# Four tiles of u move from the choice to the stretch behind the gates; scores of two groups stay in SBUF; ScalarE forms the factors of fetched slots

## The reference, cut to what matters

```python
def _peer(h, w_q, sub_keys, u_tab, v_tab):
    t = h.reshape(-1, d)                                  # 512 tokens x 1024
    qry = (t @ w_q).reshape(n_tok, 8, 2, 128)
    scores = jnp.einsum("thpd,hpkd->thpk", qry, sub_keys) # 128 keys per half
    s_top, i_top = lax.top_k(scores, 16)
    cand = s_top[:, :, 0, :, None] + s_top[:, :, 1, None, :]
    best, pos = lax.top_k(cand, 16)                       # 16 experts of 16384 per head
    gate = jax.nn.softmax(best, axis=-1)
    u = u_tab[ib]
    act = jax.nn.gelu(jnp.einsum("td,thkd->thk", tb, u))
    vv = v_tab[ib]
    return jnp.einsum("thk,thkd->td", gb * act, vv)
```

## Time and profile before

| What | us |
|---|---|
| Median of three runs (3891.67 to 3894.0) | 3893.79 |
| The profiled execution's own time | 3893.74 |
| Its span, first to last instruction | 3891.9 |
| PE busy in the span | 3771.2 (97%) |
| DVE busy | 2111.6 (54%) |
| POOL busy | 1978.0 (51%) |
| ACT busy | 1399.0 (36%) |

### The profile page before, as it was taken

One profiled execution on the slowest core, in us unless ns is written; L12 is line 12 of the kernel. 1 busy time (PEld: TensorE's weight loads), 2 busy tenths in 40 slices (PEclk: granted clock), 3 DMA queues, 4 the chain that ended last, 5 costly groups with the idle time before them and its releaser, 6 DMA issues.

```text
span 3891.9 us, 57381 instructions
## 1 busy us (share of the span) xinstructions
PE 3771.2 (97%) x21920; PEld 3290.5 (85%) x21920; DVE 2111.6 (54%) x3552; ACT 1399.0 (36%) x2131; POOL 1978.0 (51%) x1520
## 2 busy tenths in 40 slices
PE   8999999999999999999999978999999987999998
PEld 7888778888888887788877767889999987999998
DVE  3212555220322056432124855439899968999997
ACT  4222253222322133432232433334477722333332
POOL 4444424444444442444443322546644465888885
PEclk9999999999999999999999988999999998999999
DMA  3222212222222221222223210234456699888885
GB/s 140 97 97 100 77 64 98 97 97 97 95 94 94 104 88 58 92 92 97 98 103 76 44 36 24 99 108 157 154 206 209 226 381 357 326 319 324 323 319 189
DMA packets 160292, 570.02 MB, mean 146 GB/s; under 512 B 19456, under 2 KB 85248, under 8 KB 105344
## 3 DMA queue, kind: packets, MB, share of 16 engines
q1 hardware_dynamic: 49392, 351.29, 25.7%
q10 hardware_dynamic: 96912, 115.76, 8.7%
q0 software_dynamic: 13824, 100.67, 6.3%
HBM read 510.93 MB, written 56.66 MB: 146 GB/s over the span
## 4 chain that ended last, share of the span: by engine, by line
issue 34%; POOL 26%; PE 24%; DVE 13%; ACT 1%; ACTq 1%; DMA 0%; POOLq 0%; DVEq 0%
POOL w_lo L563 25%; PE bank L1362 7%; PE bank L1364 7%; PE bank L1363 7%; DVE g_buf L3043 3%; DVE hot_parts L3025 2%; DVE hot_first L3026 1%; DVE hot_parts L3031 1%; DVE bank L3126 1%; DVE late_factor L3122 1%; DVE fetched L3116 1%; POOL fetched L657 1%; ACT w_hi L730 1%; DVE gk L2601 0%; PE bank L1904 0%
## 5 line engine op out<-in xcount | busy, mean ns | idle before, releaser
L563 POOL TENSOR_TENSOR w_lo<-raw,w_hi 128x512 fp32r<-128x512 f32 x1324 | 1807.6, 1396 | 1722.4 <-ACT w_hi L730 1695.0
L1362 PE MATMUL bank<-h_hi,w_hi 128*128 128x512 f32 (+1 forms) x3232 | 1235.9, 382 | 35.8 <-POOL w_lo L563 22.9
L1363 PE MATMUL bank<-h_lo,w_hi 128*128 128x512 f32 (+1 forms) x3232 | 1222.1, 378 | 0.0
L1364 PE MATMUL bank<-h_hi,w_lo 128*128 128x512 f32 (+1 forms) x3232 | 1222.1, 378 | 0.0
L730 ACT ACTIVATE w_hi<-raw 128x2048 fp32r<-128x2048 f32 x331 | 632.7, 1911 | 832.0 <-PE bank L1364 765.4
L1362 PEld LDWEIGHTS bank<-h_hi,w_hi 128*128 128x128 f32 x3232 | 609.9, 189 | 132.5 <-POOL w_lo L563 34.1
L1363 PEld LDWEIGHTS bank<-h_lo,w_hi 128*128 128x128 f32 x3232 | 610.1, 189 | 89.7 <-issue 3.4
L1364 PEld LDWEIGHTS bank<-h_hi,w_lo 128*128 128x128 f32 x3232 | 609.4, 189 | 88.8
L1362 PE MATMUL bank<-w_mix_hi,w_hi 128*128 128x416 f32 x1024 | 363.3, 355 | 16.0 <-DVE w_mix_lo L3071 15.0
L1364 PE MATMUL bank<-w_mix_hi,w_lo 128*128 128x416 f32 x1024 | 361.8, 353 | 0.0
L1363 PE MATMUL bank<-w_mix_lo,w_hi 128*128 128x416 f32 x1024 | 358.9, 350 | 0.0
(11 more groups left out here) (430 smaller groups left out, 4416.4 us busy)
## 6 DMA issues: line engine op xcount, KB each, us to landing
raw<-weights SPq DMA_DIRECT2D x331, 1024.0 KB, 4.8
s_store<-stage ACTq DMA_DIRECT2D x64, 416.0 KB, 4.7
g_store<-g_buf ACTq DMA_DIRECT2D x8, 3328.0 KB, 15.4
g_in<-g_store ACTq DMA_DIRECT2D x32, 832.0 KB, 6.7
s_in<-s_store ACTq DMA_DIRECT2D x32, 832.0 KB, 8.2
x<-x_in SPq DMA_DIRECT2D x4, 512.0 KB, 8.5
out<-x SPq DMA_DIRECT2D x8, 256.0 KB, 2.2
q_mask<-rows ACTq DMA_DIRECT2D x6, 256.0 KB, 4.3
```

The source lines that it names most:

```text
L563: pool.tensor_tensor(w_lo[:, slot, cols], raw[:, slot, cols], w_hi[:, slot, cols].bitcast(F32), ALU.subtract).then_inc(lo_written, 1)
L1362: pe.matmul(out_ap, w_hi[:, slot, cols], m_hi, start=start, stop=False)
L1363: pe.matmul(out_ap, w_hi[:, slot, cols], m_lo, start=False, stop=False)
L1364: return pe.matmul(out_ap, w_lo[:, slot, cols], m_hi, start=False, stop=stop)
```

## The change

Three things change, all in the layer of experts.

`CHOICE_TILES` goes from 6 to 5. PE, ACT and POOL thus go through 20 tiles of u in the choice, 26 beside the gates as before, and 18 instead of 14 in the window. POOL's fetches and ACT's late gelus, which stand at fixed places of the window, are spread over it by a factor 14/18.

The scores of the last four tiles (60 to 63) are no longer stored in HBM and loaded again: ACT writes them to `s_in`, where v reads them. The host puts the u rows of groups 0 and 1 last, so that these are the scores of the first two groups of v. Loads of stored scores are left out for groups 0 and 1. The wait for the stored gates, which protects the memory under `s_in`, moves ahead of tile 60.

The product of gelu and gate for fetched slots moves from DVE (one instruction of 128x2 per step or group) to ACT (two activations of 128x1 with the gate as their scale, behind a wait for the gelu). In the groups of v, `gelu_fetched` moves from between `chain` 3 and the last `split_hi` to behind that `split_hi`.

```diff
-CHOICE_TILES = 6
+CHOICE_TILES = 5
+KEPT_GROUPS = 2
+STORED_TILES = AHEAD_TILES - 2 * KEPT_GROUPS
...
-                while s < LATE_STEPS and 2.2 + 0.7 * (s - 3) <= tile - window:
+                while s < LATE_STEPS and 2.2 + 0.7 * (s - 3) <= (tile - window) * 14 / (AHEAD_TILES - WINDOW_AT):
...
-                        if n >= 2:
+                        if 2 <= n < STORED_TILES:
...
-                    c_st.up(act.activation(stage[:, n % 2, e, :], banks[e][:, 0:DENSE], ACT.Gelu))
+                    target = stage[:, n % 2, e, :]
+                    if n >= STORED_TILES:
+                        target = s_in[:, (n - STORED_TILES) // 2, 2 * (n % 2) + e, :]
+                    c_st.up(act.activation(target, banks[e][:, 0:DENSE], ACT.Gelu))
...
+                    if g < KEPT_GROUPS:
+                        return
                     act.dma_start(s_in[:, g % 2].rearrange("p (a e) t -> p a (e t)", a=2),
...
-                    c_sg.up(act.activation(slot_gelu[:, g % 2, :], slot_score[:, g % 2, :], ACT.Gelu))
+                    act_local.step(act.activation(slot_gelu[:, g % 2, :], slot_score[:, g % 2, :], ACT.Gelu))
+                    at = g if i is None else i * 2 + g
+                    for j in range(PER_GROUP):
+                        ins = act.activation(slot_factor[:, g % 2, j:j + 1], slot_gelu[:, g % 2, j:j + 1], ACT.Copy,
+                                             scale=slot_gate[:, at, j:j + 1])
+                    c_sg.up(ins)
...
                     for e in range(EG):
                         chain(g, e, i)
-                        if e == EG - 1 and g > 0:
-                            gelu_fetched(g, i)
                         if e >= 2 and g > 0:
                             split_hi(v_tile(g - 1) + e, i, 4)
+                    if g > 0:
+                        gelu_fetched(g, i)
...
-                    c_sg.up(act.activation(late_gelu[:, s % 2, :], late_score[:, s % 2, :], ACT.Gelu))
+                    act_local.step(act.activation(late_gelu[:, s % 2, :], late_score[:, s % 2, :], ACT.Gelu))
+                    for j in range(2):
+                        ins = act.activation(late_factor[:, s % 2, j:j + 1], late_gelu[:, s % 2, j:j + 1], ACT.Copy,
+                                             scale=late_gate[:, s, j:j + 1])
+                    c_sg.up(ins)
...
-                    while s < LATE_STEPS and 3 + 1.4 * s <= row:
+                    while s < LATE_STEPS and 3 + 1.4 * s <= row * 14 / (AHEAD_TILES - WINDOW_AT):
...
-                        dve.wait_ge(sem(f"s_landed{slot}"), there if i is None else i * 16 + there)
+                        if g < KEPT_GROUPS:
+                            dve.wait_ge(sem("s_staged"), 2 * STORED_TILES + EG * (g + 1))
...
-                local.step(dve.tensor_tensor(slot_factor[:, g % 2, :], slot_gelu[:, g % 2, :], slot_gate[:, at, :],
-                                             ALU.mult))
...
-    tiles += [*u, *v]
+    tiles += [*u[KEPT_GROUPS:], *u[:KEPT_GROUPS], *v]
```

More of the change, by code:

```diff
@@ L378, in build @@
         rows = nc.dram_tensor("rows", [2, TT * 2 * GH, P], F32, kind="Internal").ap()
[L379 removed]
+        s_store = nc.dram_tensor("s_store", [STORED_TILES, NKEYS, 2, DENSE], F32, kind="Internal").ap()
         squares = [sq_ffn, sq_mix, sq_ffn, sq_ffn, sq_mix, sq_ffn, sq_second, sq_experts]
@@ L1167, in stage_row @@
                         act.wait_ge(tile_used, TABLE_AT + n + 1 if i is None else i * 2 + (TABLE_AT + n + 1))
-                    c_st.up(act.activation(stage[:, n % 2, e, :], banks[e][:, 0:DENSE], ACT.Gelu))
+                    target = stage[:, n % 2, e, :]
+                    if n >= STORED_TILES:
+                        target = s_in[:, (n - STORED_TILES) // 2, 2 * (n % 2) + e, :]
+                    c_st.up(act.activation(target, banks[e][:, 0:DENSE], ACT.Gelu))
                 def store_tile(n, i=None):
-                    target = n if i is None else act.snap(i * 2 + n)
-                    c_st.held()
-                    act.dma_start(s_store[target], stage[:, n % 2]).then_inc(s_stored[n % 2], 16)
+                    if n < STORED_TILES:
+                        target = n if i is None else act.snap(i * 2 + n)
+                        c_st.held()
+                        act.dma_start(s_store[target], stage[:, n % 2]).then_inc(s_stored[n % 2], 16)
                     split_hi(TABLE_AT + n + 2, i)
@@ L1243, in load_group @@
                     source = g if i is None else act.snap(i * 2 + g)
-                    tile = 2 * g if i is None else act.snap(i * 4 + 2 * g)
+                    tile = 2 * (g - KEPT_GROUPS) if i is None else act.snap(i * 4 + 2 * (g - KEPT_GROUPS))
                     if g >= 2 or i is not None:
@@ L1280, in looped @@
                         c_sg.loop(i, 2)
+                        act_local.loop(i, 2)
                         body(g, i)
                         body(g + 1, i)
-                    for c in (c_wh, c_sg):
+                    for c in (c_wh, c_sg, act_local):
                         c.end(trips)
@@ L1294, in experts @@
                     n = WINDOW_AT + row // 2
+                    if n == STORED_TILES and row % 2 == 0:
+                        for b in range(2):
+                            act.wait_ge(stored[b], gates_stored_of(b))
                     stage_row(n, row % 2)
@@ L1301, in experts @@
                     if row == 2 * (AHEAD_TILES - WINDOW_AT) - 3:
-                        for b in range(2):
-                            act.wait_ge(stored[b], gates_stored_of(b))
                         load_group(0)
@@ L1308, in experts @@
                 for b in range(2):
-                    act.wait_ge(s_stored[b], 16 * GROUPS)
-                looped((GROUPS - 2) // 2, 1, early_step)
+                    act.wait_ge(s_stored[b], 16 * (STORED_TILES // 2))
+                early_step(1)
+                looped((GROUPS - 4) // 2, 2, early_step)
+                early_step(GROUPS - 2)
                 early_step(GROUPS - 1)
@@ L3062, in weigh @@
                         dve.wait_ge(sem(f"gates_landed{slot}"), there if i is None else i * 16 + there)
-                        dve.wait_ge(sem(f"s_landed{slot}"), there if i is None else i * 16 + there)
+                        if g < KEPT_GROUPS:
+                            dve.wait_ge(sem("s_staged"), 2 * STORED_TILES + EG * (g + 1))
+                        else:
+                            loaded = 16 * ((g - KEPT_GROUPS) // 2 + 1)
+                            dve.wait_ge(sem(f"s_landed{slot}"), loaded if i is None else i * 16 + loaded)
                     c_wg.up(dve.tensor_tensor(chunked(weighed[:, e % 2, :]), chunked(s_in[:, slot, e, :]),
@@ L3121, in add_late @@
                     dve.wait_ge(sem("slots_gelu"), since("slots_gelu") + s + 1)
-                    local.step(dve.tensor_tensor(late_factor[:, s % 2, :], late_gelu[:, s % 2, :], late_gate[:, s, :],
-                                                 ALU.mult))
                     for j in range(2):
@@ L3137, in early_group @@
                             score_fetched(g, e, i)
-                    factor_fetched(g, i)
+                    await_factor(g, i)
                     for j in range(PER_GROUP):
@@ L3148, in looped @@
                             c.loop(i, 2 * PER_GROUP)
-                        local.loop(i, 2)
                         body(g, i)
                         body(g + 1, i)
-                    for c in (c_wg, c_wl, c_ss, c_fa, local):
+                    for c in (c_wg, c_wl, c_ss, c_fa):
                         c.end(trips)
@@ L3166, in experts @@
                 early_group(0)
-                looped((GROUPS - 2) // 2, 1, early_group)
+                early_group(1)
+                looped((GROUPS - 4) // 2, 2, early_group)
+                early_group(GROUPS - 2)
                 early_group(GROUPS - 1)
```

4 lines of the change are left out of this document (1 added, 3 removed).

## The result

The changed kernel takes 3934.75 us (median of four, 3934.73 to 3936.03) against 3892.73 for the kernel before in the same comparison: a ratio of 1.0106, 95% interval 1.0093 to 1.0119. It is slower by 1.1%, some 42 us; 28 were forecast, and the range of 3884 to 3938 holds it, by 3 us at its upper end.

What follows compares the result with a forecast made beforehand. PE was taken as full in choice, gates and v, with room only in the window. Choice -10, window +14 and v +24 gave +28 on 3893.74 us: forecast 3921 us, range 3884 to 3938.

Steps and rivals of the forecast that it cites:

- The choice: Choice of experts: four tiles leave, DVE's rounds bound it and PE waits at the turns; -10 us (-14 to -6).
- The window: Stretch between gates and v: four tiles enter, partly filling 44.4 us that are not work; +14 us (+5 to +25).
- The stand of ACT on one issue: Window, behind the gates' store: ACT stands 12.68 us on one transfer's issue; unchanged, 10.4 us of PE's loss stay.
- The end: Window's end: PE's 15.0 us rest shrinks as scores no longer travel; 7.5 us taken (4 to 15).
- The middle: Window's late steps: scores late because of DVE's slow factor; of 16.6 us lost, 5 stay (0 to 15).
- v: Groups of v: the gelu behind the last high part delays DVE's adds; 0.8 us per group, +24 us (0 to +48).
- The chain I gave: In v: adds start 3.7 us later, POOL's pieces end later, PE's next group starts 1.6 us late, half regained.
- The 0.82 us of factor that DVE loses: In v's groups: DVE's freed factor time was claimed to gain nothing, as no one waited for it.
- v did not absorb the gelu: Rival for v's groups: they absorb the moved gelu at no cost; 3898 us, chance 0.15.
- The window did not fill: Rival for the window: PE finds every tile ready, over 36 of 44 us filled; 3879 to 3887 us, chance 0.15.
- transfers did not bound it: Rival for the window: transfers at a tenth less rate bound it at 196 us; 3931 us, chance 0.10.
- The choice shrank as forecast: Answers a rival for the choice: DVE's rounds stay at 57 us, 8 us are lost; 3929 us, chance 0.08.

Runs made afterwards that it cites:

- e6: e5 with group 0's gates' load issued at tile 60 instead of 62 and its four chain steps ahead of the last tile's two rows: 3893.85 us.
- e3: Kernel before with only CHOICE_TILES 5 and the fetches and late gelus spread over the longer window; factors stay on DVE: 3905.80 us.
- e5: Changed kernel with gelu in its old place and factor on DVE in v's groups; late steps keep factors on ACT: 3898.59 us.
- e1: Changed kernel with the gelu and factors of fetched slots put back ahead of the last high part, factors still on ACT: 3916.76 us.
- e2: Kernel before with only the gelu of fetched slots moved behind the last high part, factor still on DVE: 3952.39 us.
- e9: Changed kernel with a group's two adds on DVE moved behind the next group's first two weighings: 3924.64 us.
- e11: e1 with a product of 128x2 numbers, read by no one, put on DVE ahead of the adds: 3897.79 us.
- e4: Changed kernel with v's two adds of fetched slots per group cut to 64 of 1024 columns: 3902.36 us.

## Why the prediction was right, and where it was not

**The choice.** Right: -8.4 for -10, waits of 23.8 for 23.2, the largest at the last turn. DVE's three later rounds took 53.0, 52.4 and 52.7 us where I had 56.8, 49.1 and 50.8. The sum is off by 1.4; why the single rounds came out otherwise I can't say.

**The window.** The size is right (+15.3 for +14), its parts only in sum. I had 10.4 + 7.5 + 5 = 22.9 us of rest and low clock; the trace has waits of 7.3 and 12.9 and 3.8 of low clock (PE busy for 166.8 us with 163.0 of work), 24.0 in all. The stand of ACT on one issue is there (12.30 us, PE's wait 7.3). The end was mis-sized: 12.9 us of wait, not 7.5 with its clock. The load of the gates is still issued only two rows ahead of the last product (at 3271.1, used by DVE at 3281.9), and the four chain steps stand behind the last row. e6, which moves both, takes the wait down to 3.7 us. The middle was mis-explained: PE had no wait there, where I had kept 5 us, and e3 shows that it was the wider spacing of the steps that freed them. I had named DVE's slow factor of the earlier trace rows as their cause; with that factor in place the waits went all the same. So the window's total is right partly by luck: a middle that was priced too high made up for an end that was priced too low.

**v.** Wrong in size by 10 us, 34.1 for 24, and wrong in one step. The parts:
- 31 groups gave 27.6 us (597.3 us from the first product of group 0 to that of group 31, against 569.7), 0.89 each where I had 0.8. The chain I gave is in the trace link by link.
- The last group gave 6.5 us that I had not priced: PE needs DVE's last adds, the adds come 3.9 us later, PE waits for 3.3 us and then runs at a granted clock below full (0.88 over 3889.0 to 3918.5, 1.00 before), so that it is busy for 24.9 us in that group instead of 21.7.
- The step that failed: "The 0.82 us of factor that DVE loses pays nothing: no one waited for it." No one waited, and its going changed the group all the same, by 0.5 us for the worse in the old place and 0.7 for the better in the new one:

| us per group of v | factor on DVE | factor on ACT |
|---|---|---|
| gelu ahead of the high part | 18.3 (before, e5) | 18.8 (e1) |
| gelu behind it | 19.9 (e2) | 19.2 (after) |

In the new place DVE forms its factor ahead of adds that are late already, and without it they start 0.7 us sooner. In the old place the small product keeps more of the adds clear of POOL's pieces: over the steady groups of the kernel before 37 of 57 take 1.3 us, the length that they have undisturbed, and in e1 none takes under 2.0. Without it they start 0.2 us behind DVE's last low part:

```profile
3646.93 1.43 DVE L3096 TENSOR_TENSOR w_mix_lo<-weighed,w_mix_hi 128x416 fp32r<-128x416 f32 x1 [0.65 <-ACT w_mix_hi L1265]
3648.58 4.24 DVE L3126 SCALAR_TENSOR_TENSOR fetched_sum<-fetched,slot_factor,fetched_sum 128x1024 f32<-128x1024 f32 x2 [0.22 <-DVE w_mix_lo L3096]
```

```profile
3646.59 7.36 POOL L565 TENSOR_TENSOR w_lo<-raw,w_hi 128x512 fp32r<-128x512 f32 x4
```

These are DVE's rows and POOL's in e1. The two adds take 4.24 us instead of 3.50, the four pieces 7.36 instead of 6.45. Over 27 groups the pieces take 380.3 us, 14.1 each, against 12.5 before. The two fetches of a group take 69.2 / 27 = 2.6 us, and POOL rests for (46.1 + 12.4) / 27 = 2.2, of which 1.7 is ACT's high part, which can't start before PE's end. That is 18.8 us, the group as measured, and PE waits for POOL in each of the 31: POOL is the bound. e9 ends at the same 18.8 by another way, with 384.2 / 27 = 14.2 us of pieces. e11 takes them back to 12.5 and the groups to 18.3. So the sum of v's groups came out near my number, but as the net of a place that costs 1.6 and a factor that gives 0.7 back. That the two gave 0.9 where I had 0.8 is in part luck.

One reading in the chain was off and did no harm: in the earlier trace rows DVE was not out of POOL's way. Its late factor of 128x2 numbers stood for 3.74 us beside the four pieces, which took their undisturbed 5.04 us. So the trace of the kernel before already had a case in which DVE waits out four pieces, and v has such cases too.

What is not settled is why a product of 0.69 us on average is enough in e11. The steady groups of the kernel before go through a pattern of three (18.2, 18.3, 18.5), those of e1 repeat every one. The traces show what the pattern of three holds: in one group of three, before as in e5 and e11, one of DVE's low parts takes 5.7 us because it waits out four of POOL's pieces, which then lose nothing. In e1, e9 and the changed kernel none takes over 1.7 us, and POOL's pieces bear more of the collisions. One run of e1 at 3906.4 suggests that it, too, has more than one such pattern. That a small product ahead of the adds is enough to change the pattern is shown by e11; which start leads to which pattern is not.

The Trainium skill (SBUF — State Buffer, "SBUF: two separate sides") prices a collision at the length of the instruction that holds the ports. By that the adds cost POOL their own time wherever they fall into its pieces. The runs agree in sign and roughly in size: two adds take 2.6 us where nothing holds them up, and POOL's pieces take 13.9 - 11.9 = 2.0 us per group less in e4, where the adds are short, and 14.1 - 12.5 = 1.6 less in e11, where 37 of 56 adds take 1.3 us. They don't agree where DVE waits out four pieces and not one.

**The rivals.** v did not absorb the gelu. The window did not fill ahead of its end, and transfers did not bound it: DMA was busy to 93%, less than before, and PE had no wait but the two above. The choice shrank as forecast.

## What to carry to other kernels

Where two engines' instructions lengthen each other, the length of one alone is not its price, and an engine that nobody waits for can still set the pace of the other. So ask of each edit which instructions will fall on each other, and not only who waits for whom. Taking 0.7 us of work off DVE cost 0.5 us per round here, because what stood behind it moved forward into POOL's pieces. An activation that others wait for should not stand behind one that waits for the end of a round, and the last round should be priced by itself.

## What the runs showed of the hardware

A short DVE instruction beside POOL's pieces costs by its collision and not by its size: adds of 64 columns took 911 ns on average in e4. The factor of the late steps, 128x2 numbers, took between 0.16 and 3.75 us in the window of the kernel before.

The same two engines leave each other alone where one of DVE's two sources and its target lie in PSUM, the memory that takes PE's products (`bank` in the rows). In the changed kernel 30 of the 32 late adds run beside pieces of POOL, and all 32 take 1287 to 1291 ns. In the window of e6 two adds of 128x1024 with `bank` as source and target took 2.61 us, inside four pieces of POOL that took 5.04, the length of the earlier trace rows; a piece during which DVE did nothing took 1.25 to 1.30 us in the kernel before:

```profile
3266.11 2.61 DVE L3143 SCALAR_TENSOR_TENSOR bank<-fetched,late_factor,bank 128x1024 f32<-128x1024 f32 x2 [1.47 <-ACT late_factor L1300]
```

```profile
3265.55 5.04 POOL L565 TENSOR_TENSOR w_lo<-raw,w_hi 128x512 fp32r<-128x512 f32 x4 [2.13 <-ACT w_hi L732]
```

And where they do collide they don't always take turns. In e11, DVE and then POOL:

```profile
3636.43 6.39 DVE L3096 TENSOR_TENSOR w_mix_lo<-weighed,w_mix_hi 128x416 fp32r<-128x416 f32 x2
```

```profile
3637.33 5.03 POOL L565 TENSOR_TENSOR w_lo<-raw,w_hi 128x512 fp32r<-128x512 f32 x4
```

Here DVE's second low part waited until all four pieces were through, and POOL lost nothing, where in the group of e1 above both engines were stretched. The price of a collision falls on one engine or on both, and no row here says which it will be.
